# Two layers, a second block and experts: projections read x times the norm's weight, and the norm's factor is applied to their results

## The reference, cut to what matters

```python
def rmsnorm(x, g, eps=EPS):
    xf = x.astype(jnp.float32)
    y = xf * lax.rsqrt(jnp.mean(xf * xf, axis=-1, keepdims=True) + eps)
    return (y * g.astype(jnp.float32)).astype(x.dtype)

def swiglu(h, w_gate, w_up, w_down):
    return (jax.nn.silu(h @ w_gate) * (h @ w_up)) @ w_down
...
    for l in range(DEPTH):
        x = x + 0.5 * swiglu(rmsnorm(x, g_ffn1[l]), w_ffn1_gate[l], w_ffn1_up[l], w_ffn1_down[l])
        u = rmsnorm(x, g_mix[l])
        p = u @ w_in[l]
...
        gates = jax.nn.sigmoid(u @ w_gate[l] + b_gate[l]).reshape(Bsz, S, N_BRANCHES, D)
        merged = gates[:, :, 0] * y_a + gates[:, :, 1] * y_b + gates[:, :, 2] * y_c
        x = x + merged @ w_out[l]
        x = x + 0.5 * swiglu(rmsnorm(x, g_ffn2[l]), w_ffn2_gate[l], w_ffn2_up[l], w_ffn2_down[l])
    return rmsnorm(x, g_final)
```

## Time and profile before

| | |
|---|---|
| median of 3 runs | 2912.53 us (2912.25 to 2912.93) |
| the profiled execution | 2911.06 us, span of its instructions 2909.2 us |
| busy | PE 2696.7, PEld 2164.6, DVE 1369.3, ACT 938.8, POOL 29.8 us |
| mean granted TensorE clock | 0.956 of full speed |
| DMA | 709.29 MB, 244 GB/s over the span |

### The profile page before, as it was taken

The page is one execution under the profiler, slowest core; times in us unless marked ns, Lnnn a source line. Parts: engine busy times, 40 slices in busy tenths (PEclk is TensorE's granted clock), DMA queues, the critical chain, the costliest instruction groups (busy, mean ns, idle before and its releaser), DMA issues.

```text
span 2909.2 us, 49565 instructions
## 1 busy us (share of the span) xinstructions
PE 2696.7 (93%) x19680; PEld 2164.6 (74%) x19681; DVE 1369.3 (47%) x2489; ACT 938.8 (32%) x1434; POOL 29.8 (1%) x23
## 2 busy tenths in 40 slices
PE   7998899899899889989979978889999999999995
PEld 6998579899799866989978878855555555555553
DVE  4554545555555454555555686523333333333332
ACT  4344444433333444444434534311111111111111
POOL 0000000000000000000000020000000000000000
PEclk8999899999999999999989999969999999999997
DMA  7453445345345335534544223539999999999994
GB/s 285 173 185 140 152 155 192 133 176 191 127 178 183 142 136 201 185 140 175 189 157 152 90 106 131 209 134 429 430 430 430 430 430 430 430 430 430 430 430 175
DMA packets 66670, 709.29 MB, mean 244 GB/s; under 512 B 7358, under 2 KB 7486, under 8 KB 9567
## 3 DMA queue, kind: packets, MB, share of 16 engines
q1 hardware_dynamic: 64624, 698.58, 60.2%
q0 software_dynamic: 1936, 9.17, 0.8%
HBM read 704.05 MB, written 3.67 MB: 243 GB/s over the span
## 4 chain that ended last, share of the span: by engine, by line
PE 69%; DMA 19%; DVE 8%; issue 2%; ACT 2%; DVEq 0%; POOL 0%; SPq 0%; ACTq 0%; POOLq 0%
DMA slot<-in_experts 19%; PE ps L1380 15%; PE ps L1383 15%; PE ps L1384 15%; PE ps L1863 4%; PE ps L1846 4%; PE ps L1888 3%; PE ps L1375 2%; PE ps L1901 1%; PE ps L1411 1%; PE ps L1414 1%; PE ps L1415 1%; PE ps L1452 1%; DVE u_lo L858 1%; DVE h L865 1%
## 5 line engine op out<-in xcount | busy, mean ns | idle before, releaser
L858 DVE TENSOR_TENSOR u_lo<-ring,u_hi 128x1024 fp32r<-128x1024 f32 x500 | 617.0, 1236 | 549.4 <-ACT u_hi L456 546.4
L1380 PE MATMUL ps<-hs,u_hi 128*128 128x256 f32 x2408 | 694.5, 288 | 41.7 <-DVE hs L872 40.1
L456 ACT ACTIVATE u_hi<-ring 128x1024 fp32r<-128x1024 f32 x498 | 524.9, 1056 | 587.3 <-PE ps L1380 537.1
L1383 PE MATMUL ps<-hs,u_hi 128*128 128x256 f32 x2408 | 689.5, 286 | 0.0
L1384 PE MATMUL ps<-hs,u_lo 128*128 128x256 f32 x2408 | 689.0, 286 | 0.0
L1380 PEld LDWEIGHTS ps<-hs,u_hi 128*128 128x128 f32 x2408 | 471.1, 196 | 52.6 <-DVE hs L872 43.7
L1863 PE MATMUL ps<-slot,xg 128*64 128x256 f32 x4096 | 472.2, 381 | 10.4 <-DMA slot<-in_experts 10.0
L1383 PEld LDWEIGHTS ps<-hs,u_hi 128*128 128x128 f32 x2408 | 471.1, 196 | 0.4
L1384 PEld LDWEIGHTS ps<-hs,u_lo 128*128 128x128 f32 x2408 | 470.6, 195 | 0.0
L1863 PEld LDWEIGHTS ps<-slot,xg 128*64 128x64 f32 x4096 | 290.6, 137 | 223.8 <-issue 74.3
L1888 PE MATMUL ps<-slot,eact 128*64 128x512 f32 x1024 | 249.2, 607 | 5.7 <-DMA slot<-in_experts 5.2
(11 more groups left out here) (311 smaller groups left out, 3027.4 us busy)
## 6 DMA issues: line engine op xcount, KB each, us to landing
slot<-in_experts SPq DMA_DIRECT2D x256, 1536.0 KB, 20.5
ring<-in_stream SPq DMA_DIRECT2D x184, 1536.0 KB, 6.3
slot<-in_experts SPq DMA_DIRECT2D x4, 1024.0 KB, 5.1
bias_rows<-vecs POOLq DMA_DIRECT2D x1, 2560.0 KB, 8.8
bias<-bias_rows POOLq DMA_DIRECT2D x2, 1280.0 KB, 10.4
konst<-in_konst POOLq DMA_DIRECT2D x1, 2272.0 KB, 11.8
x_tok<-in_x SPq DMA_DIRECT2D x1, 1024.0 KB, 5.3
out<-y_tok SPq DMA_DIRECT2D x1, 1024.0 KB, 4.0
```

What stands on the lines that cost most here:

```text
L456: nc.scalar.activation(u_hi[buffer_of(l, k)][:, :], raw_unit(l, k), ACT.Copy).then_inc(unit_hi, 1)
L858: nc.vector.tensor_tensor(u_lo[b][:, :], raw_unit(l, kk), u_hi[b][:, :].bitcast(F32), ALU.subtract).then_inc(unit_lo, 1)
L1380: mm = mm_(dst, hi, x_hi, start=first, stop=False, skip_group_check=True)
L1383: mm_(dst, hi, x_lo, start=False, stop=False, skip_group_check=True)
```

## The change

What it does: the projections no longer read the finished norm. ScalarE writes x * weight (a scale per partition) rounded into hs, VectorE the rest, pair of chunks by pair of chunks, each as soon as its bank of x is added. TensorE starts on them. The squares, sums, root and reciprocal follow, the sums behind the first projection pair. Whatever reads the projections' results multiplies them by the factor per token: in the feed-forward VectorE scales gate and up from PSUM (`scale_of`), then silu and product work in SBUF; VectorE scales q/k and the gates; the projections by tokens are scaled by ScalarE's copy with a factor per partition, for which TensorE turns the factor twice. Between the layers x is added bank by bank too, but the low parts follow after the copy of the parameters. The ada rows go to seven buffers, each tile waits for ScalarE's copy of the last, and all their sums are made in the projection after the attention. The bias vectors are made by four products of 33x10 by 33x512, and written by four transfers that repeat a row 128 times. Small inputs move to SP's queue, and the lambda terms into the layer loop. Squares of the second block's norms go pair by pair.

```diff
+            sp.dma_start(lp_all[:, :, :], layer_in).then_inc(par_landed, 16)
+            sp.dma_start(ring[:, 0, :], stream[0]).then_inc(tile_landed[0], 16)
+            sp.dma_start(cpad[:, :, :], cpad_in).then_inc(cpad_landed, 16)
+            sp.dma_start(relb[0:BUCKETS + 1], relb_in).then_inc(rel_landed, 16)
+            sp.dma_start(onehot[0:BUCKETS + 1], onehot_in).then_inc(rel_landed, 16)
+            for s in range(1, RING):
...
-            pool.dma_start(bias_rows.rearrange("h p v -> p h v"), vecs[:, :, :]).then_inc(rows_written, 16)
+                pool.dma_start(bias_rows[heads], vecs[heads, g, :].unsqueeze(1).to_broadcast([n, P, VEC])).then_inc(rows_written, 16)
...
+            def squares(q, sq=sq):
+                for b in range(OUTS):
+                    a.wait_ge(x_ready, q * OUTS + (b + 1))
+                    nc.scalar.activation(sq[:, 2 * b:2 * b + 2, :], x[:, 2 * b:2 * b + 2, :], ACT.Square).then_inc(sq_ready, 1)
+
+            def round_x(q, gain):
+
+                for b in range(OUTS):
+                    a.wait_ge(x_ready, q * OUTS + (b + 1))
+                    for c in (2 * b, 2 * b + 1):
+                        op = nc.scalar.activation(hs[:, c, 0, :], x[:, c, :], ACT.Copy, scale=lp[:, gain + c:gain + c + 1])
+                    op.then_inc(h_hi, 1)
...
                 def silu_of(i, g=0):
                     s = (i - 1) % 4
-                    a.wait_ge(gu_ready, f_count(l, f, i, g))
-                    nc.scalar.activation(silu[:, s, :], ps[:, s, 0:TOK], ACT.Silu).then_inc(silu_ready, 1)
-
-                round_h(l * 3 + 2 * f)
+                    a.wait_ge(gu_scaled, f_count(l, f, i, g))
+                    nc.scalar.activation(gu[:, s, 0, :], gu[:, s, 0, :], ACT.Silu).then_inc(silu_ready, 1)
+
+                round_x(l * 3 + 2 * f, (LP_FFN1, LP_FFN2)[f])
+                squares(l * 3 + 2 * f)
                 if f == 1:
                     round_unit(l, k0 + 2)
                 round_unit(l, k0 + 3)
                 round_unit(l, k0 + 4)
+                root(l * 3 + 2 * f, EPS1)
...
-                    if 7 <= u < 7 + ADA_TILES:
-                        a.wait_ge(ada_used, l * ADA_TILES + (u - 6))
-                        nc.scalar.activation(ada_sb[:, :], ps[:, 5, 0:384], ACT.Copy).then_inc(ada_row, 1)
+                    if 6 <= u < 6 + ADA_TILES:
+                        a.wait_ge(ada_used, l * ADA_TILES + (u - 5))
+                        nc.scalar.activation(ada_sb[u - 6][:, :], ps[:, 5, 0:384], ACT.Copy).then_inc(ada_row, 1)
...
+            def low_x(q, gain, b):
+
+                v.wait_ge(h_hi, q * OUTS + (b + 1))
+                for c in (2 * b, 2 * b + 1):
+                    op = nc.vector.scalar_tensor_tensor(out=hs[:, c, 1, :], in0=x[:, c, :], scalar=lp[:, gain + c:gain + c + 1],
+                                                        in1=hs[:, c, 0, :].bitcast(F32), op0=ALU.mult, op1=ALU.subtract)
+                op.then_inc(h_ready, 1)
+
+            def update(add, q, gain):
+
+                for b in range(OUTS):
+                    add(b).then_inc(x_ready, 1)
+                    if gain is not None and b > 0:
+                        low_x(q, gain, b - 1)
+                if gain is not None:
+                    low_x(q, gain, OUTS - 1)
...
+                def scale_of(i, g=0):
+                    s = (i - 1) % 4
+                    v.wait_ge(gu_ready, f_count(l, f, i, g))
+                    nc.vector.tensor_tensor(gu[:, s, :, :], ps[:, s, :].rearrange("p (a b) -> p a b", b=TOK), by_token(2), ALU.mult).then_inc(gu_scaled, 1)
...
                     for s in range(4):
                         kg = k0 + 5 + 3 * s
                         low_unit(l, kg + 3, g)
                         low_unit(l, kg + 4, g)
+                        scale_of(2 + s, g)
+                        low_unit(l, kg + 5, g)
                         act_of(2 + s, g)
-                        low_unit(l, kg + 5, g)
...
-                step(nc.vector.tensor_copy(lp[:, :], lp_all[:, l, :]))
-                ffn(l, 0, lp[:, LP_FFN1:LP_FFN1 + DC])
-                recip_std(l * 3 + 1)
-                split_norm(l * 3 + 1, lp[:, LP_MIX:LP_MIX + DC])
+                nc.vector.tensor_copy(lp[:, :], lp_all[:, l, :]).then_inc(lp_ready, 1)
+                v.wait_ge(lp_ready, l + 1)
+                for b in range(OUTS):
+                    low_x(l * 3, LP_FFN1, b)
+                ffn(l, 0, LP_MIX)
...
+                    v.wait_ge(gates_ready, l * DC + m + 1)
+                    b0 = 4 * (1 - m % 2)
+                    gates = ps[:, b0:b0 + 2, :].rearrange("p a b -> p (a b)")[:, 0:3 * TOK].rearrange("p (a b) -> p a b", b=TOK)
+                    nc.vector.tensor_tensor(sg[:, m % 2, :, :], gates, by_token(3), ALU.mult).then_inc(gates_scaled, 1)
...
-                for b in range(OUTS):
+
+                def add(b):
                     v.wait_ge(out_ready, l * OUTS + b + 1)
...
+                update(add, l * 3 + 2, LP_FFN2)
+                ffn(l, 1, None)
...
                 up_gate(0, k0)
+                sums(l * 3 + 2 * f)
                 up_gate(1, k0 + 2)
...
+            for g in range(4):
+                mm_(ps[0:BIAS_HEADS, (0, 1, 3, 4)[g], :], relb[0:BUCKETS + 1, :], onehot[0:BUCKETS + 1, g, :], start=True, stop=True).then_inc(vec_ready, 1)
+            pe.wait_ge(vec_taken, 4)
...
-                for u in range(7 + ADA_TILES + 1):
+                for u in range(UNITS + 3):
                     if u < UNITS:
                         logits(u)
                     if 2 <= u < UNITS + 2:
                         transposes(u - 2)
-                    if u >= 8:
-                        ada_sum(l * ADA_TILES + (u - 8), 5)
-                    if 7 <= u < 7 + ADA_TILES:
-                        if u >= 8:
-                            pe.wait_ge(ada_taken, l * ADA_TILES + (u - 7))
-                        ada_tile(l, ADA_TILE0 + u - 7, 5)
-                    if 3 <= u < UNITS + 3:
+                    if u >= 3:
                         weighted_values(u - 3)
+                    if 6 <= u < 6 + ADA_TILES:
+                        if u == 6:
+                            pe.wait_ge(cpad_ready, 1)
+                        else:
+                            pe.wait_ge(ada_row, l * ADA_TILES + (u - 6))
+                        ada_tile(l, ADA_TILE0 + u - 6, 5)
...
                     project_tok(l, V20 + c, c, 0, (512, 384), c == DC - 1)
+                    if c == 2:
+                        ada_sums(ADA_TILES, 5, l * ADA_TILES)
...
             ada_tile(L, 1, 3)
+            ada_tile(L, 2, 0)
+            sums(Q)
             sums(Q + 1)
```

358 lines of the change are left out of this document (169 added, 189 removed).

## The result

The changed kernel takes **2828.7 us** (median of 4 runs, 2826.8 to 2829.4) against 2912.4 (2911.9 to 2912.9): ratio 0.971, 95% interval 0.9695 to 0.9728. The gain is 84 us; the prediction gave 109.6 and 2803 us, with a range of 2790 to 2822. The direction was right, and the time lies outside the range.

What follows compares the result with a forecast made beforehand. TensorE, busy 93% of the span, was taken as the bound, its other time lying between stages. Gains less 0.9 us of transposes sum to 109.6: 2911.06 to 2801.5, forecast 2803 with the runs' median 1.5 higher; range 2790 to 2822.

Steps and rivals of the forecast that it cites:

- Start and first feed-forward stage: Kernel start: first feed-forward product at about 20.5 us against 39.72; gain 15.5 us after the sums, bounds 8 and 18.
- Feed-forward to mix: Boundary, two times: VectorE paces, TensorE stands 3.7 us, clock kept; gain 10.6 us each, 21.2 in all.
- rival C: Clock falls in the shortened boundaries and in the attention too: 2815 us, chance 0.06.
- Mix to feed-forward: Boundary, two times: adds 0 to 2 hide behind products, stand about 0.3 us; gain 13.7 each, 27.4 in all.
- Feed-forward stages at no cost: VectorE's added scaling, about 0.72 us per tile, hides behind three units of products; 0 to 1 us at starts if late.
- Between the layers: Boundary between the layers: a stand of 7.3 us, long enough for the clock to fall (2.0); gain 8.1 us.
- end of the layers: After the last layer: second sums taken as cold, 26.4 us for 32.0; gain 5.6 us, 8.7 if the clock holds.
- Attention and ada: Steps of 3.14 us shorten attention by 17.0; sums return 4.6 in the V projection; gain 12.4 a layer, 24.8.
- rival A: Ada steps stay bound by a round trip through ScalarE's copy; half the gain lost, 2815 us, chance 0.10.
- Output stage: Scaling of the gates, about 1 us per 13.3 us, taken as hidden; bound 0 to 1 us a layer.
- Second block: Norms with squares pair by pair: sums start earlier at one, run warm at the other; gain 7.9 us (3 to 9).
- Rival B: Bias-row transfers from few partitions load two DMA engines and hold up ring tiles: 10 us lost, 2813, chance 0.06.

Runs made afterwards that it cites:

- e6: Changed kernel with VectorE's four adds and remainders at the end of a feed-forward stage put ahead of the third weight unit's low part: 2823.3 us, ratio 0.9692.
- e1: Changed kernel with each tile's one-column ada sums behind a unit of their own in the second V projection, not in one block: 2823.2 us, ratio 0.9698.
- e5: Changed kernel with the mixer's adds between weight units, add 2 ahead of the last one and add 3 ahead of pair 2's remainder: 2821.1 us, ratio 0.9683.
- e8: Changed kernel with VectorE doing the new scaling of each feed-forward tile twice: 2831.3 us, ratio 0.9721.
- e3: Changed kernel with each feed-forward tile's activation ahead of the preparation of the third weight unit: 2824.1 us, ratio 0.9703.
- e7: Changed kernel with each tile's ada sums back in its attention step and TensorE waiting for VectorE's copy of them: 2840.0 us, ratio 0.9753.
- e11: Changed kernel where, for the gates' last chunk, VectorE merges the branches before preparing the next weight unit: 2824.6 us, ratio 0.9699.
- e2: Changed kernel with the mixer's adds 0 to 2 between weight units, behind the third, fifth and seventh: 2827.4 us, ratio 0.9714.
- e9: Changed kernel with relb and onehot loaded earlier, and SiLU and the four bias-vector copies moved forward on ScalarE: 2823.2 to 2828.9 us, ratio 0.9709.

## Why the prediction was wrong, point by point

**Start and first feed-forward stage, 15.5 predicted, 9.7 measured.** Two inputs were mis-sized: the landing of onehot (12.5 for 14.2; the GB/s row tells how many bytes have moved, not whose), and the four products (3.7 us for 7.0 at half clock). ScalarE's tail was right to a few tenths: table load 1.28 and SiLU 0.42, as taken from the earlier trace rows. The price of 2.66 us with its drain (the Trainium skill, ScalarE: Activation LUTs, What ACT_TABLE_LOAD costs) does not appear; the next activation starts 1.30 us after the load does. The late landing and the slow products make the 4.8 us by which the first product is late; the rest of the term is in the stage, its last down unit above all. The bounds of this term held 8, so it is inside them.

**Feed-forward to mix, 21.2 and 20.8.** The sum is right, and in the main its mechanism too: VectorE is the pacer. In layer 1 the waits are 2.12, 0.42 and 0.41 us with a small fourth, some 4 us with what a wait costs beyond its print (last section), for the predicted 3.7. The clock was taken as kept. In layer 0 it fell for 3.4 us behind the stand (0.61 and 0.53 in 224 to 228), so rival C's fall came at this place, but not its price: the stage is as long as with the clock held (e6). The argument that the clock holds because no stand is as long as the 3.5 us of the earlier trace rows was read from one boundary and does not hold. Elsewhere a fall did cost: 0.8 us behind the mixer in layer 1, 1.3 in the attention of layer 1, and the V projections (e1).

**Mix to feed-forward, 27.4 and 18.5: the step that failed.** "Here the banks of x are finished over eight units, so adds 0 to 2 hide behind products and the stand is about 0.3." The data are ready early, as said, but the adds stand in an in-order list behind a weight unit that waits for the eighth output unit. The stand is 2.2 us, then 0.35 and 0.41. With the order changed (e5) it is 0.23 and the term gains 7.5 us. The rest: the last down unit (next point), and an error on the side of the kernel before. Its rows at the starts of the first and second feed-forward stage:

```profile
39.70:43.90 4.20, 4.18 (x19) 4.18 (x20) 2.32 (x2) 1.06 (x1) 0.00 (x0) 0.50 1.03 416
563.48:569.60 6.12, 6.12 (x28) 6.12 (x29) 3.52 (x3) 2.38 (x3) 0.00 (x0) 0.50 0.30 90
```

The cold start behind the mixer cost 28 products at half clock, 2.8 us over their 3.4 warm. But the 192.0 us that served as the warm stage begin cold themselves and hold 1.9 us of the kind (66 units of 2.88 are 190.1). Against 192.0 the cold start is worth 1.0 us (193.0), where the prediction added 2.0, taken from the other boundary.

**Feed-forward stages at no cost.** For 21 of 22 tiles this was right, with room to spare (e8). The three units of cover that the price rested on are one unit at the last tile, and there TensorE waits 0.85 us, 3.4 in all (e3): here the prediction failed too, since it counted the cover once, in the middle of the loop.

**Between the layers, 8.1 and 7.8; end of the layers, 5.6 and 5.5.** Right in their parts: the branch with its copy (3.75 us of idle VectorE ahead of the copy; 3.11 in the earlier trace rows), a cold start, cold second sums of 6.6 us.

**Attention and ada, 24.8 and 20.8.** The attention is 18.0 and 17.0 us shorter, as predicted (17.0), with tiles 2.9 to 3.05 us apart: rival A is refuted. The sums came back as 7.9 and 6.3 us, not 4.6: in one block they let the clock fall (e1). Its step "come back in the V projection, which TensorE fills already" took the price of a product from a warm stretch. And the mechanism is only in part the wait that the prediction named (e7).

**Output stage, 0 to 1 us a layer allowed, 1.28 measured.** The scaling of the gates delays ScalarE by 1 us, ScalarE's rounding delays a low part, and that stands ahead of the last merge (e11).

**Second block, 7.9 and 4.9.** The two norms gained what was predicted: the sums follow the last product without the 2.06 us of idle time in the earlier trace rows, and behind the experts

```profile
2807.06 3.72 PE L1408 MATMUL ps<-sq,konst 128*128 128x256 f32 x16 [1.63 <-ACT sq L483]
```

they run warm, 3.72 us for 6.34. About 3 us were lost between, in stretches that the change doesn't touch, except for one more set of one-column sums (0.7). From its first product to the end the second block takes 1377.2 to 1381.0 us in this kernel and the twelve others with the same code for it, one trace each. Executions thus differ by as much as the 3 us that are missing; whether any of them is systematic stays open, and no experiment was made on it.

**Rival B** (bias rows written from few partitions) cost nothing: no product waits for a ring tile in the first stage, though ScalarE's rounding does twice (6.3 us in all, not at all before the change). The transfers are slow:

```profile
bias_rows<-vecs POOLq DMA_DIRECT2D x3, 512.0 KB, 14.1
...
bias_rows<-vecs POOLq DMA_DIRECT2D x1, 1024.0 KB, 70.6
```

512 KB in 14.1 us is 37 GB/s, where the ring moves 430; the rule that an outermost dimension under 16 confines a transfer to as many engines (the Trainium skill, DMA: Bandwidth & Descriptors, Rules for kernel authors) fits in direction, though other transfers ran at the same time and no run varied the dimension. The fourth, issued at 22, lands 70.6 us later, which is still far from the 290 at which the bias is wanted.

The range was too narrow because the prediction let its terms err to either side alike: most of what it had not foreseen were waits, and these only add.

## What to carry to other kernels

That the data are ready says nothing about when an in-order engine takes them up: for each "hidden" operation, name the instruction ahead of it in its list and what that one waits for. Count the cover of a pipelined loop at its last iteration too, not only in the middle. When small work is put off to a stage that is "full anyway", spread it: a block of one-column products keeps TensorE busy in the profile and lets its clock fall all the same. And before a fall of the clock is priced, see whether TensorE is the bound in that stretch: behind a slower engine half a clock can cost nothing.

## What the runs showed of the hardware

Five and a half microseconds of one-column fp32 products, with TensorE busy 2.00 of 2.00 us in every window, took the granted clock from 1.00 to 0.50, and it stayed there for about 5 us of full-width products; the same products in seven groups of 0.65 us between full-width units never did (e1). In the changed kernel a stand of 2.12 us was followed by half clock in layer 0 (0.61 and 0.53) and by full clock in layer 1 (1.00 in 924 to 934); a stand of 2.20 us at the other boundary by full clock in layer 0 (1.00 in all windows of 520 to 528) and by half clock in layer 1 (0.64 and 0.51 in 1224 to 1228). In e2 stands of 0.67 and 1.48 us were followed by half clock. The length of a stand alone doesn't tell. Nor does a fall tell what it costs. At these two boundaries, where VectorE sets the pace for the first microseconds, it lasted 3.4 us in the cases that follow. Where it came with the first product of the stage, the stage was as long as with none: 45.76 and 45.75 us of q/k stage, and 196.49 us of second feed-forward stage in layer 1 of e1 for 196.47 in layer 0 of the changed kernel. Where it came 1.0 us into the q/k stage it cost 0.34 us (46.09, in e5 and e9), and 1.9 us into the feed-forward stage 0.8 us (197.29, in layer 1 of the changed kernel). A wait of TensorE costs more than the idle time that the profile prints: at a printed 0.41 the distance from the product before to the one after is 0.69 us, where warm products stand 0.12 apart, and the first one behind it takes 0.1 more, 0.67 in all; two of these, a smaller one and the transposes make up the 2.0 us that the q/k stage of e6 has over its 43.8 us of warm products and sums.
